# Second mixer of a hybrid decoder step: chunk pairs share the products of the triangular inverse, and one product per sample state serves keys and queries

## The reference, cut to what matters

```
G = cumsum(g)
M = I + strict_lower(beta_t * (k_t . k_s) * exp(G_t - G_s))
u = M^-1 (beta v);   w = M^-1 (beta exp(G) k)
v_new = u - w S
o     = (q exp(G)) S + (lower(q k^T * decay)) v_new
S     = exp(G_end) S + (k exp(G_end - G))^T v_new
```

## Time and profile before

| | |
|---|---|
| median of 3 runs | 1878.61 us (1876.97 to 1879.4) |
| the profiled execution | 1880.24 us |
| its span, first to last instruction | 1878.4 us |
| mean granted TensorE clock | 0.955 of full |
| PE, PEld, DVE, ACT busy | 93%, 88%, 58%, 37% of the span |

### The profile page before, as it was taken

One profiled execution on the slowest core, in us unless ns is written; L12 is line 12 of the kernel. 1 busy time (PEld: TensorE's weight loads), 2 busy tenths in 40 slices (PEclk: granted clock), 3 DMA queues, 4 the chain that ended last, 5 costly groups with the idle time before them and its releaser, 6 DMA issues. The chain is left out here.

```text
span 1878.4 us, 33666 instructions
## 1 busy us (share of the span) xinstructions
PE 1748.0 (93%) x13003; PEld 1652.6 (88%) x13003; DVE 1096.1 (58%) x2081; ACT 692.2 (37%) x1166; POOL 0.4 (0%) x5
## 2 busy tenths in 40 slices
PE   6999999989999999976999999999888999999996
PEld 5888888789999999975888888888678999999996
DVE  6888888755343444546566766776624544444443
ACT  5655565332222222224445544544412322222222
POOL 0000000000000000000000000000000000000000
PEclk9999999889999999987999999999759999999997
DMA  5222222223223332221121122122102333332321
GB/s 164 78 81 77 71 69 79 58 82 90 84 85 90 89 89 85 73 56 47 46 60 50 33 60 58 34 58 58 37 12 61 89 90 90 90 88 82 87 78 48
DMA packets 257418, 134.25 MB, mean 71 GB/s; under 512 B 6698, under 2 KB 256004, under 8 KB 257348
## 3 DMA queue, kind: packets, MB, share of 16 engines
q1 hardware_dynamic: 219488, 112.49, 21.1%
q10 hardware_dynamic: 37860, 20.76, 3.8%
HBM read 121.24 MB, written 12.00 MB: 71 GB/s over the span
## 5 line engine op out<-in xcount | busy, mean ns | idle before, releaser
L419 PE MATMUL pj<-xh,w_hi 128*128 128x272 f32 x2064 | 457.0, 303 | 21.2 <-DVE w_lo L1347 13.1
L875 ACT ACTIVATE w_hi<-w_raw 128x1024 fp32r<-128x1024 f32 x209 | 220.7, 1056 | 612.7 <-PE pj L419 610.1
L419 PE MATMUL pj<-xh,w_lo 128*128 128x272 f32 x2064 | 430.7, 290 | 0.0
L419 PE MATMUL pj<-xl,w_hi 128*128 128x272 f32 x2064 | 429.7, 290 | 0.0
L419 PEld LDWEIGHTS pj<-xh,w_hi 128*128 128x128 f32 x2064 | 326.6, 191 | 44.7 <-issue 20.9
L419 PEld LDWEIGHTS pj<-xl,w_hi 128*128 128x128 f32 x2064 | 328.0, 191 | 0.0
L419 PEld LDWEIGHTS pj<-xh,w_lo 128*128 128x128 f32 x2064 | 326.5, 191 | 0.0
L419 PE MATMUL pj<-oh,w_hi 128*128 128x272 f32 x1280 | 268.7, 291 | 14.3 <-DVE ol L1403 7.0
L1347 DVE TENSOR_TENSOR w_lo<-w_raw,w_hi 128x1024 fp32r<-128x1024 f32 x209 | 254.9, 1219 | 45.1 <-ACT w_hi L875 45.0
L419 PE MATMUL pj<-oh,w_lo 128*128 128x272 f32 x1280 | 267.1, 290 | 0.0
L419 PE MATMUL pj<-ol,w_hi 128*128 128x272 f32 x1280 | 266.0, 289 | 0.0
(11 more groups left out here) (288 smaller groups left out, 1994.4 us busy)
## 6 DMA issues: line engine op xcount, KB each, us to landing
w_raw<-in_mlp_w_up_dram SPq DMA_DIRECT2D x64, 512.0 KB, 4.0
w_raw<-in_mlp_w_down_dram SPq DMA_DIRECT2D x64, 512.0 KB, 3.7
w_raw<-in_hgrn_w_in_dram SPq DMA_DIRECT2D x32, 512.0 KB, 4.0
w_raw<-in_gdn_w_in_dram SPq DMA_DIRECT2D x32, 512.0 KB, 4.1
out_dram<-S ACTq DMA_DIRECT2D x16, 512.0 KB, 3.4
S<-in_state_hgrn_dram ACTq DMA_DIRECT2D x8, 512.0 KB, 4.0
w_raw<-in_hgrn_w_out_dram SPq DMA_DIRECT2D x8, 512.0 KB, 3.6
S<-in_state_gdn_dram ACTq DMA_DIRECT2D x8, 512.0 KB, 3.9
```

The costliest lines, as they stand in the source:

```text
L419: last = mm(pj[:, s, b, 0:HALF], w[:, s, k, :], v[:, k, b * HALF:(b + 1) * HALF], start=(k == 0 and a == 0), stop=(k == KT - 1 and a == 2))
L875: f(w_hi[:, c % SPLIT], w_raw[:, slot], ACT.Copy).then_inc(w_high, 1)
```

## The change

**Pairs.** The even chunks (0 and 2) of a head are now kept in reversed order of tokens, so their triangular matrices lie on the other side of the diagonal. In a pair (even and odd chunk) the first halves of blocks of the one are then the rows that the other does not use. From m = 4 on, GpSimd builds one stationary matrix `NLm` for a pair, with alternating column blocks from the `NL` of both, ScalarE writes `Tt` in the same mixed form (`Ttm`), and one product of 128 columns takes the place of two of 64. At m = 2 the four products per step stay. At m = 64 the second product is also made once a pair.

**Samples.** At m = 8 each sample state is multiplied by its keys and queries in one product of 8 columns; the query part is kept in `VN` (step "osr") and added on VectorE to the product with the new values (step "os"). The eight products at m = 64 are gone, and the copy of step "os" on ScalarE too.

**What comes with it.** Writes that turn the even chunks are split in two: the decay rows once before the heads (`by_position`), the three silu products, and the copy of `oo`. Predicated copies into `Tm` and the copies to `Ttm` are split by even and odd chunk. `vTs` takes the place of two spare parts of `X`.

```diff
+        def by_position(out, ap):
+            o, i = blocks(out[:, 0:TP], P), blocks(ap[:, 0:TP], P)
+            return [(o[:, 0::2, ::-1], i[:, 0::2, :]), (o[:, 1::2, :], i[:, 1::2, :]), (out[:, TP:T], ap[:, TP:T])]
+        def pair_half(ap, m, odd, half):
+            return over_pairs(ap)[:, :, odd * P:(odd + 1) * P].rearrange("p q (n two m) -> p q n two m", two=2, m=m)[:, :, :, half, :]
+        def interleaved(ap, m, odd):
+            return ap.rearrange("p (q n two m) -> p q n two m", q=2, two=2, m=m)[:, :, :, odd]
+        def earlier(ap, q, m):
+            return bass.AP(ap.tensor, ap.offset + q * 2 * P + m, [ap.ap[0], [P - m, 2], [2 * m, P // (2 * m)], [1, m]])
...
+            def mix(h):                                     (GpSimd)
+                va, t = st["ga"][0], st["gr"][2]
+                for n, m in enumerate(LEVELS[2:], 1):
+                    waits = []
+                    if m == 4:
+                        waits.append((va.sem, fixed(pool, va.after("nl", h))))
+                        if not isinstance(h, int):
+                            waits.append((t.sem, fixed(pool, t.after("dSs1", h - 1))))
+                    if m >= 16:
+                        waits.append((t.sem, fixed(pool, t.after(f"x{m // 4}", h))))
...
+                    for odd in range(2):
+                        last = nc.gpsimd.tensor_copy(interleaved(NLm[n % 2], m, odd), pair_half(gd["NL"][:, 0:TP], m, odd, odd))
+                    mixed.did(last, f"m{m}")
...
-                    for c in range(NC):                     (x{m}, TensorE)
-                        cols = slice(c * P, (c + 1) * P)
-                        last = mm(rr[:, 0, c * 64:(c + 1) * 64], NL[:, cols], first_half(Tm[:, cols], m),
-                                  start=True, stop=True)
...
+                        pe.wait_ge(mixed.sem, mixed.after(f"m{m}", h))
+                        for q in range(NC // 2):
+                            last = mm(rr[:, 0, q * P:(q + 1) * P], NLm[n % 2][:, q * P:(q + 1) * P], earlier(Tm, q, m),
+                                      start=True, stop=True)
...
                     if m == 8:
-                            last = mm(rr[:, 1, b * SLEN:(b + 1) * SLEN], S0[:, b, :],
-                                      K[:, TP + b * SLEN:TP + (b + 1) * SLEN], start=True, stop=True)
+                            last = mm(rr[:, 1, 2 * b * SLEN:2 * (b + 1) * SLEN], S0[:, b, :], both, start=True, stop=True)
...
-                        mm(rr[:, 1, 0:TS], X[0:TS, VNS:VNS + P], A[0:TS, TP:T], start=True, stop=False)
-                        for b in range(NSEQ):
-                            last = mm(rr[:, 1, b * SLEN:(b + 1) * SLEN], S0[:, b, :],
-                                      qe[:, TP + b * SLEN:TP + (b + 1) * SLEN], start=False, stop=(b == NSEQ - 1))
+                        last = mm(rr[:, 1, 0:TS], vTs[:], A[0:TS, TP:T], start=True, stop=True)
...
-                        last = mm(rr[:, 0, 256 + c * 64:256 + (c + 1) * 64], Tt[:, c * P:(c + 1) * P],
-                                  X[:, c * 64:(c + 1) * 64], start=True, stop=True)
...
+                            last = mm(rr[:, 0, 256 + q * P:256 + (q + 1) * P], Ttm[:, q * P:(q + 1) * P],
+                                      X[:, q * P:(q + 1) * P], start=True, stop=True)
...
-                    last = f(Tt[:, 0:TP], rr[:, 1, :], ACT.Copy)
+                    if m < LEVELS[-2]:                      (tt{m}, ScalarE)
+                        for odd in range(2):
+                            last = f(interleaved(Ttm, 2 * m, odd), pair_half(rr[:, 1, :], 2 * m, odd, odd), ACT.Copy)
...
-                    last = pred(first_half(Tm[:, 0:TP], m), blocks(mask[:, 1, n, 0:TP // 2], m), blocks(rr[:, 0, 256:512], m))
+                    for odd in range(2):                    (pred{m}, VectorE)
+                        last = pred(pair_half(Tm[:, 0:TP], m, odd, 1 - odd), pair_cols(mask[:, 1, n, 0:TP // 2], m, odd),
+                                    pair_cols(rr[:, 0, 256:512], m, odd))
```

More of the change, by code:

```diff
@@ L90, in shape_constants @@
         cu[:, 0, n] = (row // (2 * m) == local) & (row // m % 2 == 0)
-        cu[:, 1, n] = hit & (rh[:, None] == (1 if n else 0))
+        turned = (c < TP // 2) & (c // (P // 2) % 2 == 0)
+        cu[:, 1, n] = hit & (rh[:, None] == np.where(turned, 0, 1) if n else rh[:, None] == np.where(turned, 1, 0))
     cu[:, 1, -1] = 0
@@ L184, in build @@
         QL = hg["QL"].rearrange("p (a n) -> p a n", a=2)
+        NLm = [gd["spare"][:, a * 2 * P:(a + 1) * 2 * P] for a in range(2)]
+        Ttm = gd["X"][:, TTM:TTM + 2 * P]
         gd_vbig = [gd[n][0:TS, 0:4 * P] for n in ("Tm", "spare")]
@@ L245, in build @@
                 "A", "zls", "qe", "cols2", "nbe"],
-            gr=["pred2", "vb", "pred4", "kdt", "kdts", "gate", "sr1", "pred8", "sr2", "sr3", "pred16", "pred32", "pred64",
-                "vbig", "sdec", "S0", "r1", "S1", "r2", "S2", "r3", "S3", "sn0", "sn1"],
+            gr=["pred2", "vb", "pred4", "kdt", "kdts", "gate", "osr", "sr1", "pred8", "sr2", "sr3", "pred16", "pred32", "pred64",
+                "vbig", "os", "sdec", "S0", "r1", "S1", "r2", "S2", "r3", "S3", "sn0", "sn1"],
             gf=["on", "og", "lo"],
@@ L262, in build @@
                 "K", "tm0", "zsig"],
-            gr=["x2", "tt2", "x4", "tt4", "x8", "tt8", "x16", "tt16", "rs", "x32", "tt32", "vns", "x64", "os",
+            gr=["x2", "tt2", "x4", "tt4", "x8", "tt8", "x16", "tt16", "rs", "x32", "tt32", "vns", "x64",
                 "vn0", "vn1", "vn2", "vn3", "oo", "sq"],
@@ L609, in gdn_prepare @@
                     for b in range(2):
-                        last = mm(rr[:, 2 + b, 0:HALF], cf[:, C_IND + g * P:C_IND + (g + 1) * P],
-                                  work[:, b * HALF:(b + 1) * HALF], start=True, stop=True)
+                        last = mm(rr[:, 2 + b, 0:HALF], ones[32 * g:32 * (g + 1), :],
+                                  work[32 * g:32 * (g + 1), b * HALF:(b + 1) * HALF], start=True, stop=True)
                     t.did(last, name)
@@ L747, in gdn_rec @@
                 held((s, "x64", h))
-                for c in range(NC):
-                    last = mm(rr[0:m, 0, 256 + c * m:256 + (c + 1) * m], X[:, c * m:(c + 1) * m],
-                              Tt[:, c * P + m:(c + 1) * P], start=True, stop=True)
+                for q in range(NC // 2):
+                    last = mm(rr[:, 0, 256 + q * P:256 + (q + 1) * P], X[:, q * P:(q + 1) * P], later_ends(Tt, q),
+                              start=True, stop=True)
                 t.did(last, "dt64")
@@ L1726, in gdn_prepare @@
                     dve.wait_ge(v.sem, ready)
[L1727 removed]
+                    for odd in range(2):
+                        pred(pair_half(Tt[:, 0:TP], 1, odd, odd), pair_cols(mask[:, 1, 0, 0:TP // 2], 1, odd),
+                             pair_half(NL[:, 0:TP], 1, odd, odd))
                     v.did(pred(second_half(Tt[0:TS, TP:T], 1), blocks(mask[0:TS, 1, 0, TP // 2:T // 2], 1),
```

109 lines of the change are left out of this document (78 added, 31 removed).

## The result

The changed kernel took **1866.37 us** (median of 4 runs, 1862.94 to 1868.45), the kernel before 1878.49 in the same set. The ratio is 0.9934, 95% interval 0.9917 to 0.9952: 0.66% faster, inside the predicted range and 0.6 us from the predicted 1867. The profiled execution took 1868.45 us, its span 1866.7, at a mean clock of 0.952. One later execution of it ran at a clock of 0.551 from end to end and took 2763.81 us; it is compared with nothing here.

A forecast was written before the change was run, and what follows sets the result against it. VectorE's and ScalarE's queues were taken to hide most PE time in loop heads, while head 7 has every product on the path. Loop heads -3.5, head 7 -9.9, decay rows +0.6: -12.8 from 1880.2, taken as 1867 us; range 1853 to 1880.

The forecast's parts named there:

- Rival 3: Split VectorE instructions: halves cost more than 0.08 us, 0.2 each giving 1876, or 1880 with head 7's gain halved; chance 0.13.
- Head 7: Last head, nothing else queued: every product is on the path; 7.1 and 3.5 us saved, splits cost 0.7, net -9.9.
- Loop heads: Heads 0 to 6: savings on the path of 1.39 us less added costs of 0.89, gaining 0.50 each, 3.5 in seven.
- the pairs: Loop head: of 6.1 us PE time removed, only 1.39 lies on the path, at x4, dt4, x16/dt16 and x64.
- x16 and dt16: -0.17: Loop head, before pred16: only 0.17 us was a wait for the product, so shorter products save just that.
- x32 and dt32: nothing, ScalarE's queue ends last: Loop head, tt16 to tt32: ScalarE has no gap, so shorter products there save 0 us.
- the additions: Loop head: split VectorE and ScalarE instructions and small copies add 0.89 us on the path.
- the halves: Loop head: splitting pred2, pred4, pred8, pred16 and two silu products costs 0.08 us each, 0.48 in all.
- the mixes are hidden: GpSimd's mixing copies, 0.4 us each, have 6 us or more of cover before x4 and count 0 in the sum.
- rival 2: GpSimd's copies hold up VectorE: 0.4 us each, 3.2 a head, 22 in all, giving 1889; decides from 0.23 a copy; chance 0.14.
- The clock in the loop: Loop heads: a clock fall costs 1.3 us; change left at nought, ends 1.3 less per present fall or 8 more.
- rival 4: Pair products: 128 columns cost twice 64, so pairs save nothing and the time is 1881; chance 0.02.

## Why the prediction was right

**The total** was right, 1867 against 1866.4; its parts less so, and part of the nearness is luck: the first stretch of the program gave 1.7 us by chance, head 6 took 1.0 at a lower clock, and in the next set the medians of the two kernels lay 17.2 us apart instead of 12.1. Rival 3's second figure, 1880, is 1881 by its own terms (5.6 + 0.6 - 5.0), which changes nothing.

**Head 7** (-9.9): the term was right at the clock that it assumed. In the five executions with one rise of the clock during the sample products, as the kernel before has it, head 7 up to the chunks takes 34.2 to 34.8 us against 44.3, 9.5 to 10.1 less; the one whose head 7 is the changed kernel's unaltered takes 34.5, 9.8 less. In the profiled execution of after that rise is missing, the sample products run at 1.2 GHz, and 7.6 are left; the prediction had named this bound at 1.9, and it was 2.2 (36.7 against 34.5). The 42.4 us of the earlier trace rows became 34.4 in after and 32.0 to 32.5 in those five, where 32 was forecast.

**Loop heads** (-0.50 each): an undisturbed head gained 0.6 to 0.7, from 65.2 to 64.5 or 64.6, and head 0, which was counted as one of them, 1.9. By levels, from the starts of the products x, in stretches without a fall of the clock (head 2 of before and of the kernel before with less of PE's time, head 3 of after and of the pair products twice):

| stretch | before | after | predicted change | pair products twice | before with half of them |
|---|---|---|---|---|---|
| x2 to x4 | 6.85 | 7.05 | +0.12 | 7.02 | 6.88 |
| x4 to x8 | 7.27 | 6.79 | -0.67 | 7.33 | 6.71 |
| x8 to x16 | 7.53 | 8.12 | +0.17 | 8.12 | a fall |
| x16 to x32 | 5.45 | 4.80 | -0.05 | 5.48 | 4.77 |
| x32 to x64 | 6.38 | 6.24 | 0 | 6.94 | 6.24 |
| x64 to the next x2 | 31.70 | 31.58 | -0.07 | 32.03 | a fall |

Two terms were too small. The first is the pairs: giving PE's time back costs 2.4 us a head in the changed kernel, not 1.39. The term "x16 and dt16: -0.17" was 0.65 to 0.7 in all three comparisons. "x32 and dt32: nothing, ScalarE's queue ends last" nearly held for the kernel before (0.14, with the same 6.24 in both kernels that have the shorter products), but giving the time back costs 0.7: the margin by which ScalarE's queue was the later one was small, and what the change adds to PE there has used it up (6.94 against 6.38, and the gate rows' products alone are 0.34 and 0.1 of these 0.56). The second is the additions: they cost 1.7 (66.9 against 65.2), not 0.89, and a good part of that lies in x8 to x16, 0.59 longer where 0.17 was forecast. Of these the runs separate GpSimd's 0.45, which stood in the sum as 0, 0.2 to 0.3 for the halves (0.48 forecast for those with a price), and 0.1 to 0.2 for the samples' small copies (0.18). The trace adds the gate rows' products with 32 rows, at two places 0.15 and 0.34 longer to the next start, and started 0.1 later at both (0.59 for 0.49 behind the transposes; 0.64 behind x32, where x8 gives way after 0.55); no run took them alone. Some 0.2 us stay unexplained. The two errors cancelled, which is luck.

**GpSimd**: the mixes are hidden as the prediction said, x4 never waits for them, and rival 2 had the right mechanism at a quarter of its break-even price (0.45 us over eight copies is 0.06 each, not 0.23). The Trainium skill's sentence on contention with instructions of two SBUF inputs ("GPSIMD Engine Reference", section "Key points") is borne out, on either side: three such instructions of VectorE take 0.10 to 0.14 longer beside a copy, while the convolutions, which have two such inputs too, take 0.83 each beside the copies at 1113.29 as without (2.50 and 2.49 for three), and there it is the copies that take 0.75 and 0.90 us instead of 0.3. So the sign that the prediction named for rival 2, longer convolutions, was the wrong place to look. The copies move 128 elements, not the 256 that I read out of the diff, and take 0.56 us on average, not 0.4.

**The clock in the loop** was left at nought. Of heads 0 to 5 two have a fall before and three after, which cost 1.2 us each there and 1.3, 0.4 and 0.3 here: nought in the balance, by luck. The other rivals fell: a selection in halves costs 0.05 more (rival 3), and 128 columns cost what 64 do (rival 4).

## What to carry to other kernels

Price a stretch by its granted clock before its instructions: in head 7, where PE had only the chain's own products, it was granted half its clock, and idle products in its waits gave 5 to 7 us there and, put into head 6 as well, 11 more (of which the second MLP took its 13 back), next to the 11.7 of the whole change. A queue without gaps shows which engine is last, not by how much; ask how far behind the next chain is, since a change can use that margin up, as the gate rows did here. When a total moves by 10 us or more, look first whether it moved in code that was changed: here 13 to 15 us came and went in a loop that no run touched.

## What the hardware did that was not expected

- More work made a stretch shorter: head 7 took 36.6 us at clock 0.50, 32.5 at 0.84 with 36 instructions more, 25.7 at 1.00 with fillers.
- Less work did not make the loop faster: with half of the products of x and dt left out, the kernel before had two falls of the clock in nearly every loop head (0.95) and took 65.1 us a head, next to 65.2.
- Instruction loads: 68 on the page instead of 49 to 51 went with PE idle for about 5 us at a time in the second MLP, 13 to 15 us in all, for the same code.
- VectorE beside GpSimd: 0.69 and 0.17 became 0.83 and 0.27; GpSimd's copy of 128 elements took from 0.3 to 0.9 us in the loop heads.
- After four instructions with 32 rows the next started 0.34 and 0.15 us later than after four with 128 rows (1.11 against 0.77 and 0.96 from start to start), at the same number of columns.
- Open: a kernel with the fillers and without the MLP's stall was not run; by subtraction, an estimate from the 13 us above, it would take some 1847 us.
